# Two early expert blocks around the turning of the picks: from one fp32 product to three split products

## What is computed

```python
q = (h @ peer_wq)                      # 8 heads, two halves of 128
s1, s2 = q1 @ sub_keys1.T, q2 @ sub_keys2.T
v1, i1 = top_k(s1, 16); v2, i2 = top_k(s2, 16)
top_s, pos = top_k(v1[:, None] + v2[None], 16)   # 16 picks of 256 pairs, for each head
eid = i1 * 128 + i2 at pos; gate = softmax(top_s)
a = gelu(h . peer_u[eid])
out = sum over picks of gate * a * peer_v[eid]
```

## Time and profile before

| | |
|---|---|
| median of 3 runs | 958.64 us (958.21 to 959.58) |
| the profiled execution | 957.38 us, its span 955.6 us |
| busy in the span | PE 948.3, DVE 753.0, ACT 468.7, POOL 209.6 us |
| granted clock of TensorE, mean | 1.00 |

### The profile page before, as it was taken

How to read it: one execution, slowest core, us unless ns; L and a number is a source line. 1 busy time by engine, 2 the same in 40 slices (tenths; PEclk the granted TensorE clock), 3 DMA queues, 4 the chain that set the end, 5 groups by cost and what they waited for, 6 DMA issues and landing times.

```text
span 955.6 us, 16376 instructions
## 1 busy us (share of the span) xinstructions
PE 948.3 (99%) x5324; PEld 829.7 (87%) x5324; DVE 753.0 (79%) x1453; ACT 468.7 (49%) x849; POOL 209.6 (22%) x249
## 2 busy tenths in 40 slices
PE   9999999999999999999999999999999999999998
PEld 9998899998999987888888888888888888888887
DVE  6899759998999988888677777767767767767766
ACT  6576554423899963344344344344344344344342
POOL 3075138886777720000000000000000000000000
PEclk9999999999999999999999999999999999999999
DMA  9544138726544468776665666666666666665664
GB/s 296 150 133 133 45 115 283 206 78 211 148 140 130 138 204 243 239 239 231 199 192 183 196 188 186 196 188 186 194 187 190 195 186 188 194 188 188 192 188 147
DMA packets 73593, 174.72 MB, mean 183 GB/s; under 512 B 6208, under 2 KB 39104, under 8 KB 73296
## 3 DMA queue, kind: packets, MB, share of 16 engines
q1 hardware_dynamic: 73120, 172.02, 58.2%
q0 software_dynamic: 288, 2.10, 1.1%
q10 hardware_dynamic: 144, 0.08, 0.0%
HBM read 165.26 MB, written 6.82 MB: 180 GB/s over the span
## 4 chain that ended last, share of the span: by engine, by line
PE 93%; ACT 3%; DVE 2%; DMA 2%; issue 0%; SPq 0%; POOL 0%; POOLq 0%; DVEq 0%; ACTq 0%
PE psum L1996 35%; PE psum L1976 17%; PE psum L1861 11%; PE psum L1979 9%; PE psum L1561 5%; PE psum L1830 4%; PE psum L1939 3%; PE psum L1577 2%; DMA rr<-big 1%; PE psum L1618 1%; PE psum L1739 1%; PE psum L1822 1%; PE psum L1855 1%; ACT rr L788 1%; DMA gel<-up_kept 1%; PE psum L1605 0%
## 5 line engine op out<-in xcount | busy, mean ns | idle before, releaser
L1996 PE MATMUL psum<-rr 128*128 128x512 f32 x1536 | 366.4, 391 | 0.2 <-DVE rr L1311 0.2
L1996 PEld LDWEIGHTS psum<-rr 128*128 128x128 f32 x1536 | 287.5, 188 | 60.4 <-DVE rr L1311 0.8
L1976 PE MATMUL psum<-h_all,rr 128*128 128x512 f32 x728 | 260.6, 392 | 0.0
L815 ACT ACTIVATE rr<-raw 128x1024 fp32r<-128x1024 f32 x94 | 99.7, 1061 | 295.7 <-PE psum L1996 294.5
L1279 DVE TENSOR_TENSOR rr<-raw,rr 128x1024 fp32r<-128x1024 f32 x94 | 115.2, 1225 | 125.2 <-ACT rr L815 125.2
L1979 PE MATMUL psum<-h_all,rr 128*128 128x256 f32 x728 | 188.7, 280 | 0.0
L1976 PEld LDWEIGHTS psum<-h_all,rr 128*128 128x128 f32 x728 | 136.6, 188 | 26.9
L1979 PEld LDWEIGHTS psum<-h_all,rr 128*128 128x128 f32 x728 | 136.7, 188 | 7.2
L1861 PE MATMUL psum<-t32s,raw 128*128 128x256 f32 x576 | 131.4, 379 | 0.0
L1861 PEld LDWEIGHTS psum<-t32s,raw 128*128 128x128 f32 x576 | 106.3, 190 | 12.7
L1193 DVE TENSOR_TENSOR rr<-raw,rr 128x1024 fp32r<-128x1024 f32 x90 | 109.8, 1220 | 1.4 <-ACT rr L704 1.4
(11 more groups left out here) (215 smaller groups left out, 1125.6 us busy)
## 6 DMA issues: line engine op xcount, KB each, us to landing
raw<-in_peer_v_dram SPq DMA_DIRECT2D x128, 512.0 KB, 3.5
raw<-in_peer_u_dram SPq DMA_DIRECT2D x127, 512.0 KB, 3.7
big<-in_w_in_dram SPq DMA_DIRECT2D x10, 1024.0 KB, 6.0
big<-in_peer_wq_dram SPq DMA_DIRECT2D x8, 1024.0 KB, 6.6
up_kept<-gel SPq DMA_DIRECT2D x36, 128.0 KB, 3.8
gel<-up_kept SPq DMA_DIRECT2D x34, 128.0 KB, 3.7
big<-in_w_out_dram SPq DMA_DIRECT2D x4, 1024.0 KB, 5.2
rr<-big POOLq DMA_DIRECT2D x2, 1024.0 KB, 9.8
```

Source lines behind the costliest of these rows:

```text
L815: act.activation(v_sp[s][:, 0, :], v_raw[s], ACT.Copy).then_inc(v_hi, 1)
L1976: return pe.matmul(both, ut[s][:, 0, k, :], ht[:, :, k, :], start=(k == 0), stop=(k == DK - 1))
L1996: i = pe.matmul(psum[:, 4 + 2 * t + n, :], g_sp[:, s, x, t * P:(t + 1) * P], v_sp[s][:, y, n * 512:(n + 1) * 512], start=(first and m == 0 ...
```

## The change

Blocks 13 and 14 (`SPLIT_E`), the last before the turning and the first behind it, become split products. ScalarE copies their hi (`early_high`), one ahead of the activation of block 11, one behind that of block 12, GpSimd subtracts for their lo, behind its low parts and ahead of its gated products, and TensorE does 24 fp32r matmuls for each (`early_split`), in the order hi hi, hi lo, lo hi, waiting for each part as it needs it. The parts lie in `early_sp`, which is the memory of `pairs_at`; so the second round's gated products wait until block 14 is done. `PRE` becomes 13. The wait for `p_hlo` behind the rounds is gone, since it comes earlier.

```diff
--- before.py
+++ after.py
@@ -30,8 +30,9 @@
 RING_END = EARLY - 1 - (EARLY - 2) % 3
 ACT_T = 3
 FILL0 = EARLY_TOP - 1
-PRE, TAIL = 12, 0
+PRE, TAIL = 13, 0
 EXP_AT = EARLY_TOP - 5
+SPLIT_E = (FILL0 - 1, FILL0)
 CW = 256
 
 
@@ -244,6 +245,7 @@
         v_sp = [rr[:, n:n + 2 * D].rearrange("p (a d) -> p a d", a=2) for n in (6 * D, 2 * D)]
         rows_at = [rr[:, n:n + D].rearrange("p (q n) -> p q n", q=GRP) for n in (7 * D, 8 * D)]
         pairs_at = [rr[:, n:n + 2 * D].rearrange("p (q a n) -> p q a n", q=GRP, a=2) for n in (2 * D, 4 * D)]
+        early_sp = [rr[:, n:n + 2 * D].rearrange("p (a k n) -> p a k n", a=2, k=DK) for n in (2 * D, 4 * D)]
         g_sp = rr[:, 8 * D:9 * D].rearrange("p (s a t) -> p s a t", s=2, a=2)
 
         def f(ap):
@@ -282,7 +284,7 @@
         p_ones, d_diag, pe_r, r_ev, p_t32, p_hlo = (sem(n) for n in ("p_ones", "d_diag", "pe_r", "r_ev", "p_t32", "p_hlo"))
         p_zpad, p_tpad, p_sum, d_y, d_pt = (sem(n) for n in ("p_zpad", "p_tpad", "p_sum", "d_y", "d_pt"))
         e_up, e_gel, a_iota = sem("e_up"), sem("e_gel"), sem("a_iota")
-        a_sum = sem("a_sum")
+        a_sum, eu_hi, eu_lo = sem("a_sum"), sem("eu_hi"), sem("eu_lo")
         ld_uf, d_plo, g_add, o_done = sem("ld_uf"), sem("d_plo"), sem("g_add"), sem("o_done")
         st_e = [sem(f"st_e{s}") for s in range(2)]
         ld_e = [sem(f"ld_e{s}") for s in range(2)]
@@ -709,6 +711,11 @@
                     act.wait_ge(st_e[e % 2], 16 * (e // 2))
                 act.activation(gel[:, e % 2, :], psum[:, early_bank(e), 0:SEQ], ACT.Gelu).then_inc(e_gel, 1)
 
+            def early_high(n):
+                e = SPLIT_E[n]
+                act.wait_ge(ld_t[e % 3], 16 * (e // 3 + 1))
+                act.activation(early_sp[n][:, 0], u_ring[e % 3].rearrange("p (k n) -> p k n", k=DK), ACT.Copy).then_inc(eu_hi, 1)
+
             def numbers(h):
 
                 act.wait_ge(d_top, h + 1)
@@ -764,10 +771,13 @@
             act.wait_ge(a_iota, 1)
             act.activation(psum[:, 0, 0:NK], numbers_sb, ACT.Copy).then_inc(a_iota, 1)
             for e in range(EXP_AT + 1, EARLY_TOP - 2):
+                if e == EARLY_TOP - 4:
+                    early_high(0)
                 early_gelu(e)
                 if e == EARLY_TOP - 4:
                     act.wait_ge(ld_uf, 16)
                     act.activation(ut[0][:, 0], u_first, ACT.Copy).then_inc(ut_hi, 1)
+            early_high(1)
 
             act.wait_ge(pe_pk, 1)
             turned = psum[:, 6, SEQ:2 * SEQ].rearrange("p (q j) -> p q j", j=GRP)
@@ -785,6 +795,8 @@
                     for part, scale in ((0, f(p_hi(tok, 1))), (1, picks[:, 2, tok:tok + 1])):
                         if q == 0 and part:
                             act.wait_ge(d_plo, 1)
+                        if q == 1 and j == GRP - ACT_T and not part:
+                            act.wait_ge(e_up, SPLIT_E[1] + 1)
                         i = act.activation(pairs_at[q % 2][:, j, part, :], cols[q % 2][:, j - ACT_T, :, 1], ACT.Copy, scale=scale)
                 i.then_inc(ohg_up, 1)
 
@@ -1523,6 +1535,10 @@
 
             for n in range(1, N_OUT):
                 low_part(n)
+            for n, e in enumerate(SPLIT_E):
+                pool.wait_ge(eu_hi, n + 1)
+                pool.tensor_tensor(early_sp[n][:, 1], u_ring[e % 3].rearrange("p (k n) -> p k n", k=DK), f(early_sp[n][:, 0]), ALU.subtract)\
+                    .then_inc(eu_lo, 1)
 
             def gated(q):
 
@@ -1530,6 +1546,8 @@
                 for part, p in ((0, f(p_hi(tok, n))), (1, picks[:, 2, tok:tok + n])):
                     if q == 0 and part:
                         pool.wait_ge(d_plo, 1)
+                    if q == 1 and not part:
+                        pool.wait_ge(e_up, SPLIT_E[1] + 1)
                     i = pool.tensor_tensor(pairs_at[q % 2][:, 0:n, part, :], cols[q % 2][:, :, :, 0],
                                            p.unsqueeze(2).to_broadcast([P, n, NK]), ALU.mult)
                 i.then_inc(ohp_up, 1)
@@ -1916,10 +1934,23 @@
                     queries_split(c, 1, 0, DK).then_inc(z_done, 1)
             for e in range(PH - 2, EARLY_TOP - 2):
                 early_up(e)
-            e = EARLY_TOP - 2
-            pe.wait_ge(ld_t[e % 3], 16 * (e // 3 + 1))
-            pe.wait_ge(e_gel, e - 1)
-            early_part(e, 0, DK).then_inc(e_up, 1)
+            def early_split(n):
+                e = SPLIT_E[n]
+                for a, b in ((0, 0), (0, 1), (1, 0)):
+                    if (a, b) == (0, 0):
+                        pe.wait_ge(eu_hi, n + 1)
+                        pe.wait_ge(a_hi, 4)
+                    elif b:
+                        pe.wait_ge(p_hlo, N_OUT)
+                    else:
+                        pe.wait_ge(eu_lo, n + 1)
+                    for k in range(DK):
+                        i = pe.matmul(psum[:, early_bank(e), 0:SEQ], early_sp[n][:, a, k, :], ht[:, b, k, :],
+                                      start=(a + b + k == 0), stop=(a == 1 and k == DK - 1))
+                i.then_inc(e_up, 1)
+
+            pe.wait_ge(e_gel, EARLY_TOP - 3)
+            early_split(0)
             pe.wait_ge(d_pick, PH + 1)
             pe.wait_ge(s_ev, 2 * PH)
             for a in range(3):
@@ -1944,6 +1975,10 @@
 
                 for n in range(first, last):
                     e, k = FILL0 + n // DK, n % DK
+                    if e == SPLIT_E[1]:
+                        if k == 0:
+                            early_split(1)
+                        continue
                     if k == 0:
                         early_ready(e)
                     i = early_part(e, k, k + 1)
@@ -1959,7 +1994,6 @@
                 pe.wait_ge(ohg_up, q + 1)
                 gate_half(q, 1)
                 fill(fill_end(q - 1), fill_end(q))
-            pe.wait_ge(p_hlo, N_OUT)
 
 
             def first_up(s, b):
```

## The result

The changed kernel takes 960.1 us (median of 20 executions, 958.06 to 964.03), the kernel before 957.96 (20 executions, 956.39 to 959.58): ratio 1.0027, 95% interval 1.0018 to 1.0037. It is slower by 2.1 us, 0.27%, and the interval leaves out zero. The forecast of 959.6 lies near the median, and the measured time inside the range of 957.2 to 960.2; but the forecast said 0.94 us, 0.10%, and gave 0.86 to a change within 0.2%, and the measured one is more than twice as large.

A forecast was written before the change was run, and what follows sets the result against it. TensorE, busy 948.3 of 955.6 us, was taken as the bound; +1.49 -0.55 +0.43 -0.43 gave +0.94 us on the profiled 957.38, so 958.3, and with 1.26 to the median 959.6; range 957.2 to 960.2.

The forecast's parts named there:

- The saving: Blocks 13 and 14 on TensorE: 24 split products take 2.90 us instead of 3.45, 0.55 saved each, 1.10 in all.
- The blocking: Ahead of the picks' transposes: GpSimd's subtractions hold VectorE's cast and last product, so TensorE idles 2.04 us; chance 0.44.
- Rival (a): At the picks: VectorE's casts and scalar operations don't block, all is hidden, -1.10 us, 957.5; chance 0.25.
- Rival (b): At the picks: VectorE's last product goes ahead of GpSimd's second subtraction; later waits give back the 1.10, 958.6; chance 0.22.
- the second race: Ahead of the transposes: GpSimd's second subtraction, at 235.31, starts 0.13 (or 0.04) us before VectorE's last product of the picks.
- The sum: Whole kernel: transposes +1.49, block 14 -0.55, one step more +0.43, the rounds -0.43, in all +0.94 us.
- rival (c): Behind the 2 us stall: some 3.8 us of TensorE work at half rate, 1.9 us more, 961.5; chance 0.05.
- After this one stall nothing more waits: Behind the idle time ahead of the transposes: no later work on TensorE waits, so no further time is added.
- It had 2.5 us to spare before 236.31: VectorE's last product of the picks ended at 233.81 in the kernel before, 2.5 us ahead of the transposes.

The follow-up runs named there:

- no_sub: The changed kernel with GpSimd's two subtractions cut to 8 columns each, so the low parts are left out: 956.35 us, ratio 0.9987 to the kernel before.
- dve_wq1: The changed kernel with both subtractions on VectorE instead of GpSimd and the last query weights' load issued one block earlier: 955.73 us, ratio 0.9979.
- after_fill: The changed kernel with the last query weights' load one block earlier and 16 extra, overwritten products ahead of block 13's 24: 958.12 us, ratio 1.0005.
- look_a: The changed kernel word for word, run once more for a profile: 958.09 us.
- look_b: The changed kernel word for word, run for a further profile: 958.32 us.
- after_wq1: The changed kernel with the load of the last query weights issued one block earlier: 958.50 us, ratio 1.0009 to the kernel before.
- before_wq1: The kernel before with the load of the last query weights issued one block earlier: 957.22 us, ratio 0.9990.
- before_late2: The kernel before with VectorE's last sum of the picks made three times, 5.8 us more on VectorE: 964.44 us, ratio 1.0060.
- again: The changed kernel word for word, for a second profile and more times: 963.14 us, ratio 1.0048 to the kernel before.
- only13: The changed kernel with only block 13 split and 12 steps ahead of the first round: 957.05 us, ratio 0.9992 to the kernel before.
- after: The profiled execution of the unaltered changed kernel, one of the result's 20: 963.73 us.
- after_wq3: The changed kernel with the load of the last query weights issued one block later: 965.61 us, ratio 1.0080 to the kernel before.
- before_wq3: The kernel before with the load of the last query weights issued one block later: 961.14 us, ratio 1.0030.

## Why the prediction was wrong

**The saving.** Right: 2.91 us for 24 products of 256 columns (2.90 taken, 2.86 to 2.93), and about 1.1 us gained where nothing waits (1.1 in `no_sub`, 1.05 in `dve_wq1`; 1.10 forecast).

**The blocking.** Right to 0.2 us where the load is early. Cast 2.48 us (some 2.3 forecast: to 233.67, measured to 233.87), second subtraction at 235.38 (235.31), last product 2.37, idle time 2.13 (2.04). `no_sub` shows that the length of the subtractions is the cause. Rival (a), casts that don't block, is dead. Rival (b), the second race won by VectorE, happened in one profile, `after_fill`; in `look_a`, `look_b` and `after_wq1` the race was lost by 0.26 us. The Trainium skill, page "SBUF — State Buffer", section "Who interferes with whom", says that of the two engines the one that issues first holds the shared ports for its whole instruction and the other fully blocks; these rows agree (2.48 us for a cast of 0.29).

**The sum.** Right for that mechanism: 958.3 for the profiled time against 958.09 and 958.32 in `look_a` and `look_b`; +0.94 us against 0.80 between the quick group of `after_wq1` (958.02) and `before_wq1` (957.22). Carried over to the median it was 0.7 us too high, since the median shown (958.64, of three) was that much above the one of 20 executions (957.96). From 957.96 the same sum gives 958.9, and the measured 960.1 is 1.2 above that: the forecast of 959.6 came near by luck, its base too high by 0.7 where the clock and the late load were missing.

**The step that failed: the sum put the lost clock behind the stall at nothing (rival (c), "Chance 0.05").** The prediction put TensorE idle for 2.04 us and then kept the full rate behind it ("After this one stall nothing more waits"), because waits of 0.5 to 0.7 us had done nothing. The mechanism and even the price were written down (1.9 us; 1.6 in the profile of `after_wq1`, 2.3 between its groups, 2.3 in the profile after); the chance rested on no wait longer than 0.7 us. With the load early the mean clock was down in 5 of 11 executions, the one profiled with a wait of 2.11 us; in the 20 of the result in 11; in none of the 93 of the kernel before. That idle time is the cause is shown for the long waits by `before_late2`, which adds nothing else. For the wait of 2 us it is supported by `after_fill`, none of 11, its profile without idle time, but not proven: the chip is another, and in its one profile the race had gone the other way.

**The second failure: one execution taken for all.** "It had 2.5 us to spare before 236.31" is true of executions in which the query weights land after 8.3 us. Where they land after 12 or more, the cast comes 3.8 us later while TensorE, itself held 1.41 us by the activations, starts block 13 1.2 later (233.96 against 232.76 in `look_a`): the spare time is gone before the subtractions begin. They then run back to back in front of the picks and make a wait of 3.2 us, during or right behind which the clock fell in each such profile. The trace of before showed only the early landing; its times (958.21 to 959.58, against a profiled 957.38) hinted that there was more than one kind. Together: +0.8 by the blocking alone, +2.3 more in the executions where the clock falls, and as medians 4.5 us where the load is late instead of 1.3 where it is early.

**Open.** What makes the same load land after 8.3, 9.8 or 11.6 to 12.8 us: the profiles show it in both kernels (the late one of before only in `before_late2`, itself altered), and whether the change makes the late landing more frequent isn't shown: all five executions of `again` lay at 960.2 to 963.7, where none of the eleven of `only13` on the same chip was above 957.7. How many of the 20 executions of the result had it is inferred from their times (eight at 962.4 to 964.0), not seen. Why a wait of 2.1 us comes with a lower clock in one execution and not in the next is open too.

## What to carry to other kernels

Work given to GpSimd beside VectorE is priced as a stall of VectorE of its whole length: ask who waits for VectorE there, and whether VectorE could do it itself in half the time (1.21 us against 2.37), as it could here. A stall of 2 us put before a TensorE that never waited is priced twice, as idle time and as a chance (here 5 in 11) of some 2 us more by the lower clock; work put in the hole may remove the second part. And "so much to spare" read from one execution holds for that execution: where a load is waited for upstream, move its issue up by a block and see whether the spread of times goes (956.7 to 959.1 became 956.2 to 957.8 on one chip).

## What I had not expected of the hardware

- A wait of 2.1 us was followed by a granted clock of 1.00 (`look_a`, 2.13) or by 0.50 (`after_wq1`, 2.11, in the window 240 to 242); waits of 3.18 to 3.19 us (`after`, `again`, `after_wq3`) and of 5.61 us (`before_late2`) by 0.50 in every profile that had them, and waits of 0.72 and 1.99 us (`before_wq3`) by 1.00 in its profile.
- With the clock at 0.50 for most of them, the 24 products of 256 columns take up to 4.64 us instead of 2.91.
- A scalar operation of 256 int32 elements (0.29 us alone) is held like the casts: 2.34 us behind GpSimd's subtraction in `only13`.
- A transfer of 1024 KB from one queue, issued at the same place of the program, landed after 8.3 to 8.5 us in six profiles, after 9.8 in one and after 11.6 to 12.8 in three.
